# Other rows on the partitions: how the expert weights of a mixture-of-experts layer are laid into SBUF

## The chip, the cores and the metric

The kernel runs on one NeuronCore of one Trainium2 chip. The metric is the time of one execution on the device, in microseconds (us), with all inputs in HBM at the start and all outputs in HBM at the end. Everything is f32.

## The reference, cut to what matters

One layer of a diffusion backbone over 384 tokens of width 1024 (128 context tokens, 256 latent ones). A first half mixes tokens (gated linear attention and differential attention); it is not touched here. The second half is an expert-choice mixture of experts: each of 16 experts takes the 16 context tokens and 32 latent tokens that score highest for it, and runs a SwiGLU of width 2816 on them.

```python
def ec_moe(h, w_router, w_gate, w_up, w_down):
    ...
    aff = jax.nn.softmax((xt @ w_router).astype(jnp.float32), axis=-1)
    cap = CAPACITY_FACTOR * n // N_EXPERTS
    gate, idx = lax.top_k(aff.T, cap)
    xe = jnp.take(xt, idx, axis=0)
    hid = jax.nn.silu(jnp.einsum('ecd,edf->ecf', xe, w_gate)) * jnp.einsum('ecd,edf->ecf', xe, w_up)
    ye = jnp.einsum('ecf,efd->ecd', hid, w_down) * gate[..., None].astype(h.dtype)
    out = jnp.zeros_like(xt).at[idx.reshape(-1)].add(ye.reshape(-1, D))
```

`w_gate` and `w_up` are [16][1024][2816], `w_down` is [16][2816][1024]. Both sums (over d in the first two products, over f in the third) may be taken in any order of their terms, so any row of a weight may lie on any partition, as long as the other operand has the same order.

## The kernel before, in words

The whole layer is one program with hand-written semaphores. Up to about 560 us of the span it does the token mixing, and after it the router. The rest is a loop over the 16 experts; its body is `expert` on PE and on DVE, a loop body on ACT and one on SP, which issues all loads of the weights. The last expert is written out behind the loop on PE and DVE.

**SBUF.** A ring of six quarters, each 2 x 2816 elements on every partition, holds the weights. An expert's gate and up weights are four quarters each, and they take the ring's places 0 to 5 and then 0 and 1 (`(4 * m + q) % 6`). The down weights overwrite places 2 to 5 (from `DOWN0`) once these have been read; they come in four groups (`DOWN_GROUPS`), of 3, 4, 3 and 1 of the 11 pairs of row blocks.

**Loads.** SP (lines 547 to 572) issues the loads in the order in which they are used: gate quarters, up quarters, down groups. Before each it waits until PE has used what lay in its place (`gate_used`, `up_used`, `down_used`). For gate and up (line 536) partition p takes row p * 8 + k of the matrix for k = 0 to 7, quarter q being k = 2q and 2q + 1. For down (line 544) partition p takes row p * 22 + i, for i = 0 to 21. Rows of one partition follow one another in HBM.

**PE for one expert**, `e`:

- L1008: the tokens of the expert are gathered by a product with a 0/1 matrix `sel`. The PE array is used in two halves of 64 columns (`w` = 0, 1); for w = 0 it forms one half of the features of the 48 tokens (64 slots), for w = 1 the other, on the PSUM partitions 64 to 127. Which features are "half w" is said by `h2_half`: those whose index divided by 4 is even or odd. ACT copies the result to `xe`.
- L1013: four transposes turn `xe` (columns `xe_cols[:, i, :]`, every fourth one) to have the features on the partitions. DVE copies the result to `xeT`.
- L1025: gate and up. For each k a stationary operand from `xeT` (128 features x 64 slots) and, for three blocks of columns (4, 4 and 3 times 128, `FCH`) and both halves, a moving operand from the ring. Half w takes the columns with index 2m + w, so the moving operand has a step of two elements. Gate goes to PSUM banks 0 to 2, up to 3 to 5. ACT applies silu to gate (L1297), into `hid`, while up is running; DVE multiplies it by up (L1714), one block after the other, and adds 1 to `hid_done` for each.
- L1033: 11 transposes turn `hid` (columns `hid_cols[:, i, :]`, every eleventh one). PE waits for all three blocks first, since every eleventh column is found in each. ACT copies to `hidT` (L1300).
- L1047: down, 11 x 2 x 2 products over the groups, into banks 6 and 7. DVE scales the result (L1719).
- L1055: the rows go back to their tokens by a product with `selT`; DVE adds them to the sums (L1727), and for the last expert they are added in PSUM, after L999 has brought in the sums so far.

Of the kernel before, what the change touches and what calls it, by code (L numbers as in the profile page):

```python
# [21 lines left out]
P = 128  # L22
D = 1024
KT = D // P
# [3 lines left out]
BANK = 512  # L28
# [164 lines left out]
QUARTER = 2 * FF  # L193
RING = 6 * QUARTER
FT = FF // (2 * P)
# [9 lines left out]
def trunk_layer(nc, x_prompt, x_sample, cache_k, cache_v, st_f, st_b, c, c_ctx, w_mod, b_mod, w_in,  # L205
# [5 lines left out]
    with ExitStack() as ctx:  # L211
# [28 lines left out]
        banks = ctx.enter_context(nc.psum_tensor("banks", [P, 8, BANK], F32))  # L240

        ident = kf[:, 0:P]
# [11 lines left out]
        def reg(a, n):  # L254
            return ring[:, a:a + n]
# [68 lines left out]
        h2 = rows(O4[:])  # L324
# [14 lines left out]
        hid = O2[:, 0:HALF]  # L339
        hidT = O2[:, HALF:2 * HALF].rearrange("p (i n) -> p i n", n=P)  # L340
        sel = O2[:, 2 * HALF:2 * HALF + T * SLOT].rearrange("p (t s) -> p t s", t=T)
        xe = O3[:, 0:BANK]
        xe_cols = xe.rearrange("p (n k) -> p k n", k=4)
        hid_cols = hid.rearrange("p (n i) -> p i n", i=FT)

        def h2_half(t, w):
            return h2[:, t, :].rearrange("p (n w k) -> p w n k", w=2, k=4)[:, w]

        xeT = O3[:, BANK:2 * BANK].rearrange("p (i n) -> p i n", n=P)
        yrow = O3[:, 2 * BANK:4 * BANK]  # L350
        selT = O3[:, 4 * BANK:4 * BANK + NT]
# [102 lines left out]
        hid_done = sem("hidden_ready")  # L454
# [63 lines left out]
        @block.sync  # L518
        def _(sp):
            sp.dma_start(crow[0:8, :], c_ctx.rearrange("(k p) -> k p", p=P)).then_inc(ld_c, 16)  # L520
            sp.dma_start(crow[8:16, :], c.rearrange("b (k p) -> (b k) p", p=P)).then_inc(ld_c, 16)
            sp.dma_start(kf[:], k_f).then_inc(ld_k, 16)
            sp.dma_start(x_r[:, 0, :], x_prompt[0]).then_inc(ld_x[0], 16)
            sp.dma_start(x_r[:, 1:3, :], x_sample[0].rearrange("(t p) d -> p t d", p=P)).then_inc(ld_x[1], 16)
            for n in range(len(WCHUNKS)):
                j = freed_by(SLOT_OF[n], n)
                if j is not None:
                    sp.wait_ge(job_done, j + 1)
                sp.dma_start(w_slot(n), w_chunk(n)).then_inc(wsem[SLOT_OF[n]], 16)

            sp.wait_ge(job_done, J_GB[-1] + 1)
            sp.dma_start(x_r[:, 0, :], x_prompt[0]).then_inc(ld_x2, 16)
            sp.dma_start(x_r[:, 1:3, :], x_sample[0].rearrange("(t p) d -> p t d", p=P)).then_inc(ld_x2, 16)

            def gate_up(w, e, q):
                return gate_v[w][e].rearrange("(p k) f -> p k f", p=P)[:, 2 * q:2 * q + 2, :]

            def quarter(i):
                return reg(i * QUARTER, QUARTER).rearrange("p (k f) -> p k f", k=2)

            def down(e, g):
                a, b = DOWN_GROUPS[g]
                sp.dma_start(reg(DOWN0 + 2 * a * D, 2 * (b - a) * D).rearrange("p (i d) -> p i d", d=D),
                             w_down[0][e].rearrange("(p i) d -> p i d", p=P)[:, 2 * a:2 * b, :]).then_inc(land_d[g], 16)


            wait_family(sp, F_M)
            for q in range(4):
                if q == 3:
                    wait_job_copied(sp, J_WO[-1])  # L550
                sp.dma_start(quarter(q), gate_up(0, 0, q)).then_inc(land_g[q], 16)
            for q in range(4):
                if q >= 2:
                    sp.wait_ge(gate_used, q - 1)
                sp.dma_start(quarter((4 + q) % 6), gate_up(1, 0, q)).then_inc(land_u[q], 16)
            for g in range(4):
                if g == 0:
                    sp.wait_ge(gate_used, 4)
                else:
                    sp.wait_ge(up_used, min(g, 2))  # L560
                down(0, g)
            with sp.Fori(1, NE) as e:

                for q, (used, n) in enumerate(((up_used, 1), (up_used, 0), (down_used, 3), (down_used, 2))):
                    sp.wait_ge(used, e * 4 - n)
                    sp.dma_start(quarter(q), gate_up(0, e, q)).then_inc(land_g[q], 16)
                for q, (used, n) in enumerate(((down_used, -1), (down_used, 0), (gate_used, 1), (gate_used, 2))):
                    sp.wait_ge(used, e * 4 + n)
                    sp.dma_start(quarter((4 + q) % 6), gate_up(1, e, q)).then_inc(land_u[q], 16)
                for g, (used, n) in enumerate(((gate_used, 4), (up_used, 1), (up_used, 2), (up_used, 2))):  # L570
                    sp.wait_ge(used, e * 4 + n)
                    down(e, g)
            for t in range(T):
                sp.wait_ge(f_ready, t + 1)
                dst = y_prompt[0] if t == 0 else y_sample[0, (t - 1) * P:t * P, :]
                sp.dma_start(dst, x_r[:, t, :]).then_inc(stored, 16)
            sp.wait_ge(stored, 16 * T)
            sp.wait_ge(kv_stored, 32)
            sp.wait_ge(gla_st, 16 * 2 * GH)
# [112 lines left out]
        def _(pe):  # L692
# [309 lines left out]
            def expert(e, last=False):  # L1002

                pe.wait_ge(sel_ready, e * T + T)
                pe.wait_ge(acc_done, e * 6 + 6)
                for t in range(T):
                    for w in range(2):
                        x = pe.matmul(banks[64 * w:64 * w + 64, 3, :], sel[:, t, :], h2_half(t, w),  # L1008
                                      start=(t == 0), stop=(t == T - 1))
                x.then_inc(xe_done, 1)  # L1010
                pe.wait_ge(xe_cp, e + 1)
                for i in range(4):
                    x = pe.transpose(banks[:, 4, i * P:(i + 1) * P], xe_cols[:, i, :], ident)  # L1013
                x.then_inc(xet_done, 1)
                pe.wait_ge(xet_cp, e + 1)

                for m, (land, used) in enumerate(((land_g, gate_used), (land_u, up_used))):
                    for q in range(4):
                        pe.wait_ge(land[q], e * 16 + 16)
                        w4 = reg(((4 * m + q) % 6) * QUARTER, QUARTER).rearrange("p (k m w) -> p k w m", k=2, w=2)  # L1020
                        for kk in range(2):
                            k = 2 * q + kk
                            for b, (i0, i1) in enumerate(FCH):
                                for w in range(2):
                                    x = pe.matmul(banks[64 * w:64 * w + 64, 3 * m + b, 0:(i1 - i0) * P],  # L1025
                                                  xeT[:, k % 4, 64 * (k // 4):64 * (k // 4) + 64],
                                                  w4[:, kk, w, i0 * P:i1 * P], start=(k == 0), stop=(k == KT - 1))
                        x.then_inc(used, 1)

                pe.wait_ge(hid_done, e * 3 + 3)  # L1030
                for b, (i0, i1) in enumerate(FCH):
                    for i in range(i0, i1):
                        x = pe.transpose(banks[:, b, (i - i0) * P:(i - i0 + 1) * P], hid_cols[:, i, :], ident)  # L1033
                    x.then_inc(hidt_done, 1)

                if last:
                    rows_so_far(range(3, 6))
                pe.wait_ge(hidt_cp, e * 3 + 3)
                wd = reg(DOWN0, FF // P * D).rearrange("p (i w d) -> p i w d", w=2, d=D)
                for g, (i0, i1) in enumerate(DOWN_GROUPS):  # L1040
                    if last and g == 1:
                        rows_so_far(range(3))
                    pe.wait_ge(land_d[g], e * 16 + 16)
                    for i in range(i0, i1):
                        for dc in range(2):
                            for w in range(2):
                                x = pe.matmul(banks[64 * w:64 * w + 64, 6 + dc, :], hidT[:, i, 64 * w:64 * w + 64],  # L1047
                                              wd[:, i, w, dc * BANK:(dc + 1) * BANK], start=(i == 0), stop=(i == FT - 1))
                    x.then_inc(down_used, 1)

                pe.wait_ge(selT_ready, e + 1)
                pe.wait_ge(y_cp, e * 2 + 2)
                for t in range(T):
                    for dc in range(2):
                        pe.matmul(banks[:, 2 * t + dc, :], selT[:, t * P:(t + 1) * P], yrow[:, dc * BANK:(dc + 1) * BANK],  # L1055
                                  start=not last, stop=True, skip_group_check=last).then_inc(comb_done, 1)
# [715 lines left out]
```

## Time and profile before

| | |
|---|---|
| three runs | 1917.98, 1918.8, 1919.66 us; median 1918.8 |
| the profiled execution | 1917.98 us, span 1916.2 us |
| mean granted clock of TensorE | 0.968 |
| PE busy | 1709.6 us, 89% |
| DMA, all queues | 642.58 MB, mean 335 GB/s over the span |

The span reaches from the first to the last instruction; the time of an execution is 1.8 us longer. In the rows, PE is the matmuls and PEld the loads of their stationary operands, DVE the vector engine, ACT the scalar engine and SPq the queue of SP, which issues the loads. An f32 matmul stands in the trace as two records. "DMA share" is the mean busy share of the core's 16 DMA engines. A packet is one contiguous run that one of them moves; each DMA ends with 16 small ones that write its semaphore, which the view counts under 512 B.

### The profile page before, as it was taken

To read this page: it belongs to the slowest core of one execution; us is meant where nothing else is said; L and a number is where in the kernel's file an instruction comes from. 1 tells how busy PE (TensorE), PEld (TensorE's weight loads), DVE (VectorE), ACT (ScalarE), POOL (GpSimd) and SP (SyncE) were. 2 spreads that over 40 slices of the span, in tenths; PEclk is the share of its full clock that TensorE was granted. 3 is DMA by queue.
4 is the path that set the end of the run, shared out by engine and by line. 5 is a ranking of instruction groups with operands and counts; after the bars stand their busy time and mean duration, and the time that the engine had idled before them with its cause. 6 is when DMAs were issued, how large, how long until landed. Compare 5 with 4: busy or idle time off the path is not lost.

```text
span 1916.2 us, 18332 instructions
## 1 busy us (share of the span) xinstructions
PE 1709.6 (89%) x7569; PEld 797.6 (42%) x7569; DVE 502.9 (26%) x934; ACT 282.7 (15%) x557; POOL 85.6 (4%) x136
## 2 busy tenths in 40 slices
PE   4899997999996989989999888998889989889996
PEld 1446776777764333333333233332333333333332
DVE  2166566776447010110101101011010110101103
ACT  1221132445213010001000000000000000000000
POOL 3001031112001000000000000000000000000000
PEclk9999998999998999999999999999999999999999
DMA  8683243314466799999999999999999999999995
GB/s 280 251 292 89 71 127 99 88 45 136 144 246 257 319 429 431 431 431 433 426 431 431 431 430 429 430 432 431 431 428 428 432 432 432 428 430 430 431 428 213
DMA packets 59479, 642.58 MB, mean 335 GB/s; under 512 B 4929, under 2 KB 5073, under 8 KB 31793
## 3 DMA queue, kind: packets, MB, share of 16 engines
q1 hardware_dynamic: 55232, 629.83, 79.4%
q0 software_dynamic: 4208, 12.24, 2.0%
q8 instruction: 25, 0.41, 0.1%
q14 instruction: 14, 0.11, 0.0%
HBM read 638.34 MB, written 3.71 MB: 335 GB/s over the span
## 4 chain that ended last, share of the span: by engine, by line
PE 66%; DMA 22%; DVE 8%; issue 2%; ACT 1%; SPq 0%; POOL 0%; DVEq 0%; ACTq 0%
PE banks L1025 24%; DMA ring<-in_w_exp_down 15%; PE banks L754 13%; PE banks L1047 11%; PE banks L1055 4%; DMA ring<-in_w_exp_up 4%; PE banks L760 3%; PE banks L1008 2%; PE banks L728 2%; DMA ring<-in_w_mod 2%; PE banks L882 1%; DVE slot_parts L1471 1%; PE banks L811 1%; DMA ring<-in_w_in 1%; DVE O L1719 1%
## 5 line engine op out<-in xcount | busy, mean ns | idle before, releaser
L1025 PE MATMUL banks<-ring,O 128*64 128x512 f32 (+1 forms) x3072 | 640.2, 575 | 28.2 <-DMA ring<-in_w_exp_up 14.5
L1025 PEld LDWEIGHTS banks<-ring,O 128*64 128x64 f32 x3072 | 229.1, 134 | 431.1 <-issue 403.0
L1047 PE MATMUL banks<-ring,O 128*64 128x512 f32 x1408 | 328.1, 623 | 24.3 <-DMA ring<-in_w_exp_down 14.4
L1047 PEld LDWEIGHTS banks<-ring,O 128*64 128x64 f32 x1408 | 101.8, 144 | 241.0 <-issue 194.9
L1714 DVE TENSOR_TENSOR O<-O,banks 128x512 f32<-128x512 f32 (+1 forms) x48 | 28.0, 639 | 651.6 <-PE banks L1025 651.6
L754 PE MATMUL banks<-slot_parts,X_parts 128*128 128x512 f32 x576 | 161.3, 421 | 9.6 <-issue 9.6
L1719 DVE TENSOR_TENSOR O<-banks,O 128x512 f32<-128x512 f32 x32 | 20.6, 686 | 388.6 <-PE banks L1047 388.6
L754 PEld LDWEIGHTS banks<-slot_parts,X_parts 128*128 128x128 f32 x576 | 107.4, 194 | 35.6 <-issue 10.4
L1055 PE MATMUL banks<-O 128*128 128x512 f32 x192 | 86.6, 601 | 22.4 <-DVE O L1719 22.4
L760 PE MATMUL banks<-ring,H 128*128 128x512 f32 x192 | 84.5, 595 | 0.0
L1471 DVE TENSOR_TENSOR slot_parts<-ring,slot_parts 128x512 fp32r<-128x512 f32 x128 | 81.0, 689 | 4.0 <-ACT slot_parts L1094 2.8
L1294 ACT ACTIVATE O<-banks 128x512 f32<-128x512 f32 x16 | 9.6, 597 | 470.1 <-PE banks L1008 470.1
L754 PE MATMUL banks<-slot_parts,H_parts 128*128 128x512 f32 x288 | 78.7, 390 | 0.0
L1300 ACT ACTIVATE O<-banks 128x512 f32<-128x512 f32 (+1 forms) x48 | 24.4, 560 | 355.7 <-PE banks L1033 355.5
L1297 ACT ACTIVATE O<-banks 128x512 f32<-128x512 f32 (+1 forms) x48 | 23.5, 563 | 327.0 <-PE banks L1025 327.0
L1727 DVE TENSOR_TENSOR X<-X,banks 128x512 f32<-128x512 f32 x90 | 61.8, 687 | 31.2 <-PE banks L1055 31.2
L1055 PEld LDWEIGHTS banks<-O 128*128 128x128 f32 x192 | 35.2, 190 | 74.7 <-issue 40.6
L754 PEld LDWEIGHTS banks<-slot_parts,H_parts 128*128 128x128 f32 x288 | 54.1, 188 | 11.7
L1008 PE MATMUL banks<-O 128*64 128x512 f32 x192 | 47.3, 629 | 12.4 <-DVE X L1727 11.8
L1033 PE MATMUL banks<-kf,O 128*128 128x128 f32 x176 | 29.4, 324 | 31.1 <-DVE O L1714 31.1
L760 PEld LDWEIGHTS banks<-ring,H 128*128 128x128 f32 x192 | 35.8, 190 | 45.8 <-issue 45.8
L728 PE MATMUL banks<-H,ring 128*128 128x384 f32 x128 | 45.1, 510 | 6.0 <-DMA ring<-in_w_in 5.9
(256 smaller groups left out, 1169.2 us busy)
## 6 DMA issues: line engine op xcount, KB each, us to landing
ring<-in_w_exp_gate SPq DMA_DIRECT2D x64, 2816.0 KB, 30.3
ring<-in_w_exp_up SPq DMA_DIRECT2D x64, 2816.0 KB, 26.1
ring<-in_w_exp_down SPq DMA_DIRECT2D x32, 3072.0 KB, 23.5
ring<-in_w_exp_down SPq DMA_DIRECT2D x16, 4096.0 KB, 28.1
ring<-in_w_in SPq DMA_DIRECT2D x16, 2048.0 KB, 9.8
ring<-in_w_mod SPq DMA_DIRECT2D x12, 2048.0 KB, 15.4
ring<-in_w_exp_down SPq DMA_DIRECT2D x16, 1024.0 KB, 32.4
ring<-in_w_proj_a SPq DMA_DIRECT2D x2, 2048.0 KB, 7.8
```

Source lines behind the costliest of these rows:

```text
L728: x = pe.matmul(out[:, 0:NT], w[:, k, i * P:(i + 1) * P], hT[:, k, :], start=(k == 0), stop=(k == KT - 1))
L754: x = pe.matmul(out, a[:, k, i * P:(i + 1) * P], w[:, k, :], start=(n == 0 and k == 0), stop=(n == 2 and k == KT - 1))
L760: x = pe.matmul(out, src[:, k, i * P:(i + 1) * P], w[:, k, :], start=(k == 0), stop=(k == KT - 1))
L1008: x = pe.matmul(banks[64 * w:64 * w + 64, 3, :], sel[:, t, :], h2_half(t, w), start=(t == 0), stop=(t == T - 1))
L1025: x = pe.matmul(banks[64 * w:64 * w + 64, 3 * m + b, 0:(i1 - i0) * P], xeT[:, k % 4, 64 * (k // 4):64 * (k // 4) + 64], w4[:, kk, w, i0 * ...
L1033: x = pe.transpose(banks[:, b, (i - i0) * P:(i - i0 + 1) * P], hid_cols[:, i, :], ident)
L1047: x = pe.matmul(banks[64 * w:64 * w + 64, 6 + dc, :], hidT[:, i, 64 * w:64 * w + 64], wd[:, i, w, dc * BANK:(dc + 1) * BANK], start=(i == ...
L1055: pe.matmul(banks[:, 2 * t + dc, :], selT[:, t * P:(t + 1) * P], yrow[:, dc * BANK:(dc + 1) * BANK], start=not last, stop=True, skip_group ...
L1471: dve.tensor_tensor(low[:, k, :], w[:, k, :], high[:, k, :].bitcast(F32), ALU.subtract).then_inc(w_split, 1)
L1714: dve.tensor_tensor(hid[:, i0 * P:i1 * P], hid[:, i0 * P:i1 * P], banks[:, 3 + b, 0:(i1 - i0) * P], ALU.mult).then_inc(hid_done, 1)
L1719: dve.tensor_tensor(yrow[:, cs], banks[:, 6 + dc, :], g2s[:, cs], ALU.mult).then_inc(y_cp, 1)
L1727: dve.tensor_tensor(dst, dst, banks[:, n, :], ALU.add).then_inc(acc_done, 1)
```

## The change

The rows of the expert weights are laid on the partitions the other way round: row k * 128 + p of gate and up on partition p, and row i * 128 + p of down. With it every operand that has to follow that order changes: half w of the features is w * 512 to w * 512 + 511; `xe` and `hid` are transposed in blocks of 128 contiguous columns; of gate and up's columns half w takes the blocks of 128 with an even or odd number. As a block of `hid` columns is complete now when its own product is done, PE waits for the three products one by one, each just ahead of the transposes that need it.

```diff
-        xe_cols = xe.rearrange("p (n k) -> p k n", k=4)
-        hid_cols = hid.rearrange("p (n i) -> p i n", i=FT)
-
-        def h2_half(t, w):
-            return h2[:, t, :].rearrange("p (n w k) -> p w n k", w=2, k=4)[:, w]
...
             def gate_up(w, e, q):
-                return gate_v[w][e].rearrange("(p k) f -> p k f", p=P)[:, 2 * q:2 * q + 2, :]
+                return gate_v[w][e].rearrange("(k p) f -> p k f", p=P)[:, 2 * q:2 * q + 2, :]
...
-                             w_down[0][e].rearrange("(p i) d -> p i d", p=P)[:, 2 * a:2 * b, :]).then_inc(land_d[g], 16)
+                             w_down[0][e].rearrange("(i p) d -> p i d", p=P)[:, 2 * a:2 * b, :]).then_inc(land_d[g], 16)
...
-                        x = pe.matmul(banks[64 * w:64 * w + 64, 3, :], sel[:, t, :], h2_half(t, w),
+                        x = pe.matmul(banks[64 * w:64 * w + 64, 3, :], sel[:, t, :], h2[:, t, w * BANK:(w + 1) * BANK],
                                       start=(t == 0), stop=(t == T - 1))
...
-                    x = pe.transpose(banks[:, 4, i * P:(i + 1) * P], xe_cols[:, i, :], ident)
+                    x = pe.transpose(banks[:, 4, i * P:(i + 1) * P], xe[:, i * P:(i + 1) * P], ident)
...
-                        w4 = reg(((4 * m + q) % 6) * QUARTER, QUARTER).rearrange("p (k m w) -> p k w m", k=2, w=2)
+                        w4 = reg(((4 * m + q) % 6) * QUARTER, QUARTER).rearrange("p (k i w n) -> p k i w n", k=2, w=2, n=P)
...
-                                                  w4[:, kk, w, i0 * P:i1 * P], start=(k == 0), stop=(k == KT - 1))
+                                                  w4[:, kk, i0:i1, w, :], start=(k == 0), stop=(k == KT - 1))
...
-                pe.wait_ge(hid_done, e * 3 + 3)
                 for b, (i0, i1) in enumerate(FCH):
+                    pe.wait_ge(hid_done, e * 3 + b + 1)
                     for i in range(i0, i1):
-                        x = pe.transpose(banks[:, b, (i - i0) * P:(i - i0 + 1) * P], hid_cols[:, i, :], ident)
+                        x = pe.transpose(banks[:, b, (i - i0) * P:(i - i0 + 1) * P], hid[:, i * P:(i + 1) * P], ident)
```

## Rows read from the trace of the kernel before

**Rows 1.** The page: DMA share and rate in 40 slices, packets, chain by engine.

```profile
DMA  8683243314466799999999999999999999999995
GB/s 280 251 292 89 71 127 99 88 45 136 144 246 257 319 429 431 431 431 433 426 431 431 431 430 429 430 432 431 431 428 428 432 432 432 428 430 430 431 428 213
DMA packets 59479, 642.58 MB, mean 335 GB/s; under 512 B 4929, under 2 KB 5073, under 8 KB 31793
...
PE 66%; DMA 22%; DVE 8%; issue 2%; ACT 1%; SPq 0%; POOL 0%; DVEq 0%; ACTq 0%
```

**Rows 2.** Windows: stretch, length, busy of PE, PEld, DVE, ACT, POOL; clock, DMA share, GB/s.

```profile
214.50:221.50 7.00, 7.00 (x38) 5.37 (x38) 0.97 (x4) 2.10 (x7) 0.00 (x0) 1.00 0.97 282
499.30:504.30 5.00, 4.80 (x19) 3.51 (x20) 1.11 (x2) 0.00 (x0) 0.00 (x0) 1.00 1.01 385
...
700.00:1870.00 1170.00, 1047.71 (x4686) 378.24 (x4686) 129.56 (x237) 89.48 (x131) 0.00 (x0) 0.98 1.00 430
...
1880.00:1890.00 10.00, 10.00 (x40) 3.45 (x42) 0.00 (x0) 0.00 (x0) 0.00 (x0) 1.00 0.83 352
```

**Rows 3.** Timeline of ACT, the copy of `xe` in four experts: start, duration, idle before.

```profile
785.74 0.60 ACT L1294 ACTIVATE O<-banks 128x512 f32<-128x512 f32 x1 [28.29 <-PE banks L1008]
861.62 0.60 ACT L1294 ACTIVATE O<-banks 128x512 f32<-128x512 f32 x1 [28.29 <-PE banks L1008]
...
1342.32 0.60 ACT L1294 ACTIVATE O<-banks 128x512 f32<-128x512 f32 x1 [31.16 <-PE banks L1008]
1422.73 0.60 ACT L1294 ACTIVATE O<-banks 128x512 f32<-128x512 f32 x1 [30.72 <-PE banks L1008]
```

**Rows 4.** Waits over 700 to 1850 us: in total, times, longest.

```profile
PEld banks L1047 <- DMA ring<-in_w_exp_down: 32.2, 22, 3.1
...
PEld banks L1025 <- DMA ring<-in_w_exp_up: 24.4, 21, 2.2
```

**Rows 5.** DMA view of 501 to 504, 547.8 to 549.8 and 1100 to 1180 us.

```profile
DMA packets 587, 1.20 MB, mean 401 GB/s; under 512 B 0, under 2 KB 0, under 8 KB 587
...
DMA packets 202, 0.82 MB, mean 408 GB/s; under 512 B 3, under 2 KB 3, under 8 KB 202
...
DMA packets 1719, 34.40 MB, mean 430 GB/s; under 512 B 192, under 2 KB 192, under 8 KB 192
```

**Rows 6.** Timeline of PE: the first gate matmuls, and the last expert's end.

```profile
633.54 39.83 PE L1025 MATMUL banks<-ring,O 128*64 128x512 f32 x192 [0.86 <-DVE O L1705]
...
1863.45 5.18 PE L1025 MATMUL banks<-ring,O 128*64 128x512 f32 x24 [1.38 <-DMA ring<-in_w_exp_up]
...
1882.67 13.95 PE L1047 MATMUL banks<-ring,O 128*64 128x512 f32 x64
```

**Rows 7.** Timeline of all engines, 1141 to 1180 us, one expert from up to the next.

```profile
1141.50 0.14 PEld L1025 LDWEIGHTS banks<-ring,O 128*64 128x64 f32 x2 [0.31 <-issue]
1141.84 0.14 PEld L1025 LDWEIGHTS banks<-ring,O 128*64 128x64 f32 x2 [0.20 <-issue]
...
1144.97 1.75 DVE L1714 TENSOR_TENSOR O<-O,banks 128x512 f32<-128x512 f32 x3 [41.28 <-PE banks L1025]
...
1146.78 1.61 PE L1033 MATMUL banks<-kf,O 128*128 128x128 f32 x11 [1.95 <-DVE O L1714]
1147.57 1.47 ACT L1300 ACTIVATE O<-banks 128x512 f32<-128x512 f32 x3 [22.60 <-PE banks L1033]
...
1149.09 5.37 PE L1047 MATMUL banks<-ring,O 128*64 128x512 f32 x24 [0.70 <-ACT O L1300]
...
1150.43 0.14 PEld L1047 LDWEIGHTS banks<-ring,O 128*64 128x64 f32 x2 [0.29 <-issue]
...
1179.90 2.79 PE L1008 MATMUL banks<-O 128*64 128x512 f32 x12 [0.78 <-DVE X L1727]
```

**Rows 8.** Lines by form, 700 to 1850 us: busy and mean ns of a weight load.

```profile
L1055 PEld LDWEIGHTS banks<-O 128*128 128x128 f32 x180 | 33.0, 190 | 70.0 <-issue 35.9 <-DVE O L1719 34.1
...
L1033 PEld LDWEIGHTS banks<-kf,O 128*128 128x128 f32 x154 | 21.6, 215 | 37.1 <-DVE O L1714 37.1
```

## The prediction, made before the changed kernel was run

> **What bounds the kernel now.** I read the page first, for where the time goes. Expert loads fill the last two thirds of the span: the DMA digits stand at 9 from slice 17 on and the rate stays at 426 to 433 GB/s. But the page's chain gives PE 66% of the span and DMA 22% [rows 1], so the page alone can't say which of the two sets the pace. The windows answer it: over 700 to 1870 us the 16 DMA engines are busy for a share of 1.00 at 430 GB/s, and PE for 1047.71 of 1170 us, 90% [rows 2]. A queue that is never empty is a bound; an engine that rests for a tenth isn't.
>
> The starts of the ACT copy of `xe`, one for each expert, check it [rows 3]. From 785.74 to 861.62 an expert takes 75.88 us: the loads are still ahead from the start and PE sets the pace. From 1342.32 to 1422.73 it takes 80.41 us. An expert's weights are 3 x 1024 x 2816 x 4 bytes = 34.60 MB, and 34.60 MB at 430 GB/s is 80.5 us. So after the first few experts the loads set the period, and PE, which needs 75.9, waits 4.5 us for them in each. The waits name them: `in_w_exp_down` and `in_w_exp_up` before L1047 and L1025, 32.2 and 24.4 us on the weight loads [rows 4]. What shortens PE's work inside an expert is worth nothing there; what lengthens a load is paid in full.
>
> **The packets.** The number of bytes and of DMA issues does not change. What changes is the length of a contiguous run in HBM, and so the number of packets. Before, partition p reads rows p*8+2q and p*8+2q+1 of gate or up, which lie one behind the other: one packet of 22.5 KB. Afterwards it reads row k*128+p for two k: two packets of 11 KB. For down, partition p reads 6, 8, 6 or 2 rows in one piece now (24, 32, 24, 8 KB, by `DOWN_GROUPS`) and afterwards that many pieces of 4 KB. An engine serves 8 partitions, so per expert: gate and up go from 64 to 128 packets per engine, down from 32 to 176. That is 208 more, 64 and 144.
>
> The trace of before shows what a packet costs beyond its bytes. Dense stretches [rows 5]: in 1100:1180 there are 1719 packets less 192 completion writes, so 1527 of 22.5 KB on average; 16 engines x 80 us / 1527 = 838 ns each. In 501:504 587 packets of 2 KB, so 81.8 ns each, 401 GB/s. In 547.8:549.8 199 of 4 KB, so 160.8 ns each, 408 GB/s. A line through the 2 KB and the 22.5 KB point has 36.9 ns per KB of 1000 bytes and leaves 6.2 ns per packet; one through the 4 KB and the 22.5 KB point leaves 10.3 ns. These are my bounds for one more packet in a full queue. I take 7 ns, near the 2 KB row, which rests on three times as many packets. An expert then takes 208 x 7 ns = 1.5 us longer (1.3 to 2.1).
>
> The Trainium skill gives a smaller price (DMA: Bandwidth & Descriptors, section Why small descriptors are slow): about 3 cycles per packet beside one cycle for each 32 bytes. By that an 11 KB packet loses 0.4% more than a 22.5 KB one and a 4 KB packet 2% more than a long one, 0.8 us per expert, and the end would come near 1928 us. The rows at 2 and 4 KB ask for more than that, and I go by them.
>
> **Where the extra time counts.** The stream runs without a gap from the release of the first gate quarter of expert 0 at about 638 us (PE starts on it at 633.54 [rows 6], and a quarter of gate or up takes it 5 us). The six quarters loaded before that were waiting in any case. Up to the last up quarter of expert 15, which PE waits for at 1863.45 [rows 6], it holds 122 quarters and 15 downs: 122 x 8 + 15 x 144 = 3136 more packets on each engine. 3136 x 7 ns = 22.0 us (19.4 to 32.3).
>
> **What PE gains.** Four edits, all for PE.
> - L1025's moving operand has a step of two elements now; afterwards it is four runs of 128. The trace has two records for each f32 matmul, and their weight loads come in pairs. Two pairs stand 0.14 + 0.31 = 0.45 us apart for 512 columns and 0.14 + 0.20 = 0.34 for 384, against 0.14 + 0.29 = 0.43 for 512 at L1047, whose operand is contiguous [rows 7]; 384 would be 0.32 at that pace. Per k there are four such steps of 512 and two of 384: 6 x 0.02 = 0.12, x 16 (8 k, gate and up) = 1.9 us per expert. The last up quarter holds two of the 16 k: 0.25 us.
> - `hid_done` is waited for block by block. Now PE stands still while DVE multiplies three blocks: DVE starts at 1144.97, the transposes at 1146.78, ACT's first copy at 1147.57, the down matmuls at 1149.09 [rows 7]. With the first block turned at once, the transposes start after one product of 0.69 us, about 1145.7; they run behind DVE and ACT's copies (1.47 us together) behind them, the last block is ready at 1146.72, turned by 1147.4 and copied by 1148.1. That is 0.95 us earlier.
> - `hid_cols` (step 11) and `xe_cols` (step 4) become contiguous. Loads for the transposes take 215 ns against 190 for the 128-column loads of L1055 [rows 8], so 15 x 0.025 = 0.4 us at most; 0.2 of it behind the last up load, nothing below.
> - `h2_half` reads groups of four now and halves afterwards. Its 12 records take 2.79 us as they are [rows 7], the pace of a contiguous operand; nothing.
> Sum 3.1 to 3.3 us: PE would need 72.8 in place of 75.9 per expert. In the period this is hidden by the loads; PE only waits longer, 9 us instead of 4.5. It shows twice. At the start, the first quarter is released 0.25 us sooner. At the end, the chain from the last up quarter to the last down matmul is PE work alone, 1863.45 to 1882.67 + 13.95 = 1896.6 [rows 6], with no wait for down: 0.25 + 0.95 + 0.2 = 1.4 us shorter. Down has to be there in time: the stream ends near 1888 (352 GB/s in 1880:1890 is 3.5 MB, then empty [rows 2]). Afterwards it ends at 1888.2 + 22.0 + 1.0 - 0.25 = 1911, while PE wants the last group 1.8 us before 1917, at 1915. It is still hidden, with 4 us to spare; at 10 ns per packet too.
>
> **Sum.** 22.0 - 0.25 - 1.4 = +20.3 us. The profiled execution took 1917.98 us for a span of 1916.2, so 1938.3; the median of the runs is 0.8 above that execution. I say 1938.5 us, 1.0% slower.
>
> **Rivals.**
> A. Packets cost nothing in a full queue: the reads of the next packet start while the last is written, and only bytes count. For it: the DMA share is a little over 1 in dense stretches, 1.01 at 2 KB [rows 2], so packets do overlap. Against: the spacing worked out above has that overlap in it already, and it is still 5 to 7% wide of the long packets' rate. It would give -1.7 us, 1917. By the rule of the Trainium skill that 512 bytes are enough for line rate (DMA: Bandwidth & Descriptors, Specifications) this is what should come; the rows at 2 KB and 4 KB disagree.
> B. PE is the bound, as its 66% of the chain suggests, and its 3.1 us per expert come off: 15 x 3.1 = 47 us, 1871. It decides only where the loads of an expert take less than PE's 75.9 us; at 80.4 that is far. The first five experts, where PE did set the pace, only hand their time back to the wait for the loads.
> C. HBM reads adjacent rows faster, since a whole DMA is one stretch of 1.4 or 0.5 to 1 MB afterwards. It would have to bring 430 GB/s to over 437 before the packets' price is taken off to turn the sign (20.3 of some 1250 us are 1.6%); at 440 it ends near 1910. Against it: `in_w_proj_a` has neighbouring partitions 4 KB apart, and such loads reach 385 to 401 GB/s [rows 2, 5].
> D. The new order of rows collides in HBM. `in_w_in` runs at 282 GB/s over 7 us where loads of the same size from `in_w_proj_b` and `in_w_out` make 385 [rows 2], so the layout in HBM can cost. If only down fell to 385 GB/s, 11.5 MB would take 30.0 in place of 26.8 us: 3.2 per expert in place of my 1.0, 1971 in all; at 282 GB/s 2135. Against it: down's pitch afterwards is that of `in_w_proj_a` and the loads of x, which ran dense at 401 and 408.
> PE's clock is a smaller matter: its granted mean is 0.98 [rows 2], more waiting may halve it more often, and there are 9 us of room in each period. In the last 33 us one stretch of a few us at half speed costs 2 to 3.
>
> **How the numbers follow.** The forecast with its bounds: from half the lower price (3 ns, should the 2 KB stretch hold gaps of its own) to the upper one and 3 us for the clock, so 9.4 - 1.7 to 32.3 - 1.7 + 3 on 1918: 1926 to 1951, chance 0.74. A 0.10 (1914 to 1922), B 0.02, C 0.05, D and anything else above 1951 0.09. A measurement of this kernel tells 0.2%, 3.8 us, from no change. Slower is all of the forecast and D; A is mostly within 0.2%; B and C are faster: 0.84, 0.09, 0.07. The range 1924 to 1951 leaves out A, B, C and D: at most 2 in 10, the forecast's own edge of 2 us with them.
>
> **What would show it.** DMA packets about 112,700 in place of 59,479 [rows 1] (3328 more on each of 16 engines); the share still 1.00 from 700 us on, with 420 to 425 GB/s in place of 430; 81.9 us between `xe` copies in the middle; L1025's loads 0.43 apart; PE's waits for `in_w_exp_down` and `in_w_exp_up` doubled; the wait before L1033 down from 1.95 to under 1 us. I am wrong if the rate stays at 430 (A), passes 437 (C), or falls under 415 (D), or if PE still takes 75.9 us where it isn't waiting for a load.

## The result, and the profile after

The changed kernel takes 1948.4 us (median of 4 runs, 1946.3 to 1949.2), the kernel before in the same job 1918.5. The ratio is 1.0152, 95% interval 1.0138 to 1.0167: 29.9 us slower, where 20 were forecast.

The page of the changed kernel, the lines that answer to [rows 1]:

```profile
span 1946.4 us, 18362 instructions
...
DMA  8673242224285899999999999999999999999995
GB/s 275 252 292 94 61 135 82 87 56 159 105 313 221 350 426 416 423 420 417 425 416 424 418 419 423 417 426 416 420 422 417 425 416 421 420 417 426 416 422 220
DMA packets 112726, 642.58 MB, mean 330 GB/s; under 512 B 4928, under 2 KB 5072, under 8 KB 76848
...
PE 66%; DMA 25%; DVE 6%; issue 2%; ACT 1%; SPq 0%; DVEq 0%; ACTq 0%
```

DMA stands at 9 from slice 17 on as before, and the rate under them is 416 to 426 GB/s instead of 426 to 433. The bytes are the same to the last digit, the packets are nearly twice as many. The chain still gives PE 66%; it was no sign of the bound before and is none now.

Windows of the changed kernel, columns as in [rows 2]:

```profile
700.00:1870.00 1170.00, 1002.65 (x4548) 357.00 (x4548) 125.10 (x229) 88.76 (x128) 0.00 (x0) 0.97 1.01 420
...
1910.00:1920.00 10.00, 9.43 (x39) 2.98 (x39) 0.00 (x0) 0.00 (x0) 0.00 (x0) 1.00 0.99 394
1920.00:1930.00 10.00, 8.52 (x36) 2.88 (x33) 1.29 (x2) 0.00 (x0) 0.00 (x0) 1.00 0.03 14
```

PE is busy for 45 us less in the same 1170 us [rows 2], and the end comes later all the same. About half of the 45 is work that now lies outside the window, as each expert takes 2.4% longer (25 of 1047.71 us); the rest is what the edits saved. The stream of loads ends at about 1919.4 (394 GB/s over the last full window, at 420 while it ran), where it ended near 1888 before.

Timeline of ACT in the changed kernel, the copy of `xe` in experts 0, 1, 2 and 15 (as [rows 3]):

```profile
632.17 0.60 ACT L1288 ACTIVATE O<-banks 128x512 f32<-128x512 f32 x1 [9.12 <-PE banks L1002]
705.09 0.60 ACT L1288 ACTIVATE O<-banks 128x512 f32<-128x512 f32 x1 [28.29 <-PE banks L1002]
784.65 0.60 ACT L1288 ACTIVATE O<-banks 128x512 f32<-128x512 f32 x1 [34.35 <-PE banks L1002]
...
1855.83 0.60 ACT L1288 ACTIVATE O<-banks 128x512 f32<-128x512 f32 x1 [34.69 <-PE banks L1002]
```

From expert 2 on the loads set the period: (1855.83 - 784.65) / 13 = 82.40 us against 80.41 [rows 3]. The 208 further packets of an engine cost 1.99 us, 9.6 ns each. The 80.41 is one period; ten of them in the kernel before give (1825.00 - 1020.65) / 10 = 80.44, and with that it is 9.4 ns:

```profile
1020.65 0.60 ACT L1294 ACTIVATE O<-banks 128x512 f32<-128x512 f32 x1 [30.24 <-PE banks L1008]
...
1825.00 0.60 ACT L1294 ACTIVATE O<-banks 128x512 f32<-128x512 f32 x1 [31.34 <-PE banks L1008]
```

Expert 0 took 72.92 us, the 72.8 that PE was expected to need; the lead of the loads, which lasted four experts before, is gone within expert 1.

DMA view of the changed kernel over 1303 to 1313 us (gate or up, 11 KB) and 1321 to 1331 us (down, 4 KB):

```profile
DMA packets 396, 4.27 MB, mean 427 GB/s; under 512 B 17, under 2 KB 17, under 8 KB 17
...
DMA packets 1016, 4.10 MB, mean 410 GB/s; under 512 B 16, under 2 KB 16, under 8 KB 1016
```

Less the completion writes that is 16 x 10 us / 379 = 422 ns for 11 KB and 16 x 10 / 1000 = 160.0 ns for 4 KB. The 4 KB row of [rows 5] had said 160.8. One packet more or less in so short a window moves these spacings by 1.1 and 0.2 ns, so the price of a packet is better read from the periods.

Waits of the changed kernel over 700 to 1850 us (as [rows 4], and the wait ahead of the transposes, 37.1 us in [rows 8]):

```profile
PEld banks L1041 <- DMA ring<-in_w_exp_down: 72.8, 16, 5.3
...
PEld banks L1019 <- DMA ring<-in_w_exp_up: 47.6, 27, 2.5
...
PEld banks L1027 <- DVE O L1708: 24.3, 28, 1.6
```

Both waits for weights have doubled: PE's saved time is in them. Timeline of the changed kernel at the hand-over from up to down, and at the end:

```profile
1305.76 0.15 PEld L1019 LDWEIGHTS banks<-ring,O 128*64 128x64 f32 x2 [0.28 <-issue]
...
1306.94 0.15 PEld L1019 LDWEIGHTS banks<-ring,O 128*64 128x64 f32 x2 [0.17 <-issue]
...
1322.55 1.75 DVE L1708 TENSOR_TENSOR O<-O,banks 128x512 f32<-128x512 f32 x3 [40.96 <-PE banks L1019]
1323.29 0.42 PEld L1027 LDWEIGHTS banks<-kf,O 128*128 128x128 f32 x4 [1.56 <-DVE O L1708]
1323.30 1.61 PE L1027 MATMUL banks<-kf,O 128*128 128x128 f32 x11 [0.89 <-DVE O L1708]
...
1325.62 5.37 PE L1041 MATMUL banks<-ring,O 128*64 128x512 f32 x24 [0.71 <-ACT O L1294]
...
1335.38 15.54 PE L1041 MATMUL banks<-ring,O 128*64 128x512 f32 x64 [4.40 <-DMA ring<-in_w_exp_down]
...
1894.11 4.94 PE L1019 MATMUL banks<-ring,O 128*64 128x512 f32 x24 [1.84 <-DMA ring<-in_w_exp_up]
...
1903.96 5.37 PE L1041 MATMUL banks<-ring,O 128*64 128x512 f32 x24
...
1919.69 7.09 PE L1041 MATMUL banks<-ring,O 128*64 128x512 f32 x32 [0.57 <-DMA ring<-in_w_exp_down]
```

Pairs of weight loads stand 0.15 + 0.28 = 0.43 and 0.15 + 0.17 = 0.32 us apart; from DVE's start to the first down matmul it is 3.07 us, 4.12 in [rows 7]. PE won in the loop what it was to win, and stood still for 4.40 us a little later.

### The profile page after: what moved, and what is told of

The parts are those of the page before. It is cut to its first block, busy times and chain, and to the rows that moved or that the text cites. A ratio compares the mean times of both kernels' runs of the same rounds, so it can differ in the third digit from the quotient of the medians.

```text
span 1946.4 us, 18362 instructions
## 1 busy us (share of the span) xinstructions
PE 1689.8 (87%) x7569; PEld 784.7 (40%) x7569; DVE 502.7 (26%) x934; ACT 283.5 (15%) x557; POOL 85.6 (4%) x136
## 2 busy tenths in 40 slices
DMA packets 112726, 642.58 MB, mean 330 GB/s; under 512 B 4928, under 2 KB 5072, under 8 KB 76848
## 3 DMA queue, kind: packets, MB, share of 16 engines
q1 hardware_dynamic: 108480, 629.83, 80.4%
## 4 chain that ended last, share of the span: by engine, by line
PE 66%; DMA 25%; DVE 6%; issue 2%; ACT 1%; SPq 0%; DVEq 0%; ACTq 0%
DMA ring<-in_w_exp_down 23%; PE banks L1019 21%; PE banks L1041 13%; PE banks L748 13%; PE banks L754 4%; PE banks L1049 4%; PE banks L1002 2%; PE banks L722 2%; DMA ring<-in_w_mod 2%; PE banks L876 1%; PE banks L716 1%; DVE slot_parts L1465 1%; PE banks L805 1%; DMA ring<-in_w_in 1%; DVE O L1713 1%
## 5 line engine op out<-in xcount | busy, mean ns | idle before, releaser
L1019 PE MATMUL banks<-ring,O 128*64 128x512 f32 (+1 forms) x3072 | 613.8, 558 | 46.8 <-DMA ring<-in_w_exp_up 33.1
L1041 PE MATMUL banks<-ring,O 128*64 128x512 f32 x1408 | 340.2, 643 | 71.2 <-DMA ring<-in_w_exp_down 60.5
L748 PEld LDWEIGHTS banks<-slot_parts,X_parts 128*128 128x128 f32 x576 | 107.6, 194 | 35.6 <-issue 10.3
L695 PE MATMUL banks<-kf,O 128*128 128x128 f32 x144 | 25.5, 303 | 21.3 <-DVE O L1388 12.6
```

The lines of the kernel that those rows point to most:

```text
L695: x = pe.transpose(banks[:, 2 + b % 2, i * P:(i + 1) * P], src, ident)
L748: x = pe.matmul(out, a[:, k, i * P:(i + 1) * P], w[:, k, :], start=(n == 0 and k == 0), stop=(n == 2 and k == KT - 1))
```

## Experiments

Three theories for the 30 us. One: each packet has a fixed price in a queue that is never empty. Two: HBM gives adjacent rows more slowly, and the cost goes with the bytes so read. Three: SP's queue is blocked. The last came from the trace. The issues of down by their line, first in the kernel before (a timeline row, and the durations in ns, least, median and most), then in the changed one:

```profile
1364.62 10.89 SPq L543 DMA_DIRECT2D ring<-in_w_exp_down  x4
...
L543 SPq DMA_DIRECT2D ring<-in_w_exp_down x64: 327/333/432, 653.6 to 1857.8; - x64
```

```profile
1300.39 28.34 SPq L537 DMA_DIRECT2D ring<-in_w_exp_down  x4
...
L537 SPq DMA_DIRECT2D ring<-in_w_exp_down x64: 368/1654/11936, 653.5 to 1898.7; - x64
```

From the first to the end of the last, the four issues of an expert take 28 us instead of 11 (most of the 11 is waiting between them), and a single one lasts up to 11.9 us where 0.43 was the most.

The differences below are the stated ratio applied to some 1920 us. The kernel before moved by one or two us from job to job (medians 1918.5 to 1920.3), and among the profiled executions the first copy of `xe` starts anywhere between 630.1 and 634.4 us, before any of the edits can act; a difference of 1 or 2 us in one profile is within that. The period between copies of `xe` does not depend on where the experts begin.

### The rows of gate and up alone

```diff
-                return gate_v[w][e].rearrange("(p k) f -> p k f", p=P)[:, 2 * q:2 * q + 2, :]
+                return gate_v[w][e].rearrange("(k p) f -> p k f", p=P)[:, 2 * q:2 * q + 2, :]
```
with `h2[:, t, w * BANK:(w + 1) * BANK]` and `xe[:, i * P:(i + 1) * P]` as the operands that follow from it.

> The new row order for gate and up alone (with the operands h2 and xe that must follow it); down as before. Theory 1, a fixed price per packet in a queue that is never empty: the two profiles give (82.38 - 80.41) us / 208 packets = 9.5 ns. Here 64 more packets per engine and expert: period 81.0 us, 976 packets x 9.5 ns = 9.3 us in all, 1928 us. Theory 2, the order of rows in HBM costs by the byte: gate and up are two thirds of the bytes and take two thirds of the 30 us, 1938 us. Theory 3, the descriptors of down that block SP's queue (issues of up to 11.9 us) are the cause: nothing here, 1918 us.

1929.5 us, ratio 1.0044 (1.0027 to 1.0061), 8.4 us (9.2 by the medians). Timeline of ACT (copies of `xe` seven experts apart) and of SP:

```profile
1188.24 0.60 ACT L1294 ACTIVATE O<-banks 128x512 f32<-128x512 f32 x1 [31.16 <-PE banks L1008]
...
1755.39 0.60 ACT L1294 ACTIVATE O<-banks 128x512 f32<-128x512 f32 x1 [31.16 <-PE banks L1008]
...
1292.74 10.89 SPq L543 DMA_DIRECT2D ring<-in_w_exp_down  x4
```

The period is 81.02 us, 0.61 for 64 packets: 9.5 ns (0.58 and 9.1 ns from 80.44). Two thirds of the bytes in the new order made less than a third of the loss, so theory two falls by its size. SP's issues of down take 10.89 us as before (and none of gate and up lasts over 0.40), and the loss is there, so theory three explains no part of this.

### The down side alone

Everything else of the change: `(i p) d` for down, the column blocks, the contiguous transposes and the waits for `hid_done` block by block.

> The rest of the change alone: down in 4 KB rows, the new column blocks, contiguous transposes, the wait for hid block by block; gate and up rows as before. Theory 1 (price per packet, 9.5 ns): 144 more per engine and expert, period 81.8 us, 15 x 144 x 9.5 ns = 20.5 us, less 1.7 for PE at start and end, plus 0.6 for the last down group: 1938 us. Theory 2 (bytes in the new order): one third of 30 us, 1928 us. Theory 3 (SP blocked by down's descriptors): the whole 30 us, 1948 us.

1939.3 us, ratio 1.0097 (1.0081 to 1.0114), 18.6 us. Timeline of ACT, seven experts apart:

```profile
1112.37 0.60 ACT L1294 ACTIVATE O<-banks 128x512 f32<-128x512 f32 x1 [34.52 <-PE banks L1008]
...
1684.86 0.60 ACT L1294 ACTIVATE O<-banks 128x512 f32<-128x512 f32 x1 [34.60 <-PE banks L1008]
```

The period is 81.78 us, 1.37 for 144 packets: 9.5 ns (9.3 from 80.44). The two halves of the change give 8.4 + 18.6 = 27.0 us; the whole gave 29.9, within the three intervals.

### PE's edits with the old loads

All edits of the change except the two load patterns. The products are of rows that don't belong together; their number and size are those of the kernel.

> All of PE's edits with the loads of the kernel before, so the operands don't belong to one another and the products are of other rows; the work is the same in size. Theory 1: the loads keep their 80.4 us per expert, PE needs 3 us less and waits 3 us more in each; only the start (0.25) and the end (1.4) show, 1916.8 us. Rival: PE sets the pace after all, 15 x 3 us less, 1873 us. Rival of the other sign: longer waits halve PE's clock more often, or the faster releases order the loads worse: above 1920 us.

1917.1 us, ratio 0.9981 (0.9972 to 0.9991): 3.6 us less, with 1.7 to 5.4 in the interval, where 1.6 was expected. Timeline of PE at its end, and of ACT eight experts apart:

```profile
1866.79 4.95 PE L1025 MATMUL banks<-ring,O 128*64 128x512 f32 x24 [0.92 <-DMA ring<-in_w_exp_up]
...
1884.72 13.95 PE L1047 MATMUL banks<-ring,O 128*64 128x512 f32 x64
...
1106.63 0.60 ACT L1294 ACTIVATE O<-banks 128x512 f32<-128x512 f32 x1 [34.80 <-PE banks L1008]
...
1749.03 0.60 ACT L1294 ACTIVATE O<-banks 128x512 f32<-128x512 f32 x1 [33.69 <-PE banks L1008]
```

The last stretch, 1866.79 to 1898.67, is 31.9 us against 33.2 [rows 6]: 1.3 of the 3.6. The period is 80.30, the loads' own. PE is busy for 1022 of the 1170 us from 700 on, 25 less than before [rows 2]. So 3 us of PE's work per expert are worth next to nothing while the loads fill the queue, and PE is not the bound. Where the other 2 us are is open; they are the size of the spread between executions, and the profiled one, at 1920.1 us, is among the slower.

### Short packets in the old order

```diff
-                sp.dma_start(reg(DOWN0 + 2 * a * D, 2 * (b - a) * D).rearrange("p (i d) -> p i d", d=D),
-                             w_down[0][e].rearrange("(p i) d -> p i d", p=P)[:, 2 * a:2 * b, :]).then_inc(land_d[g], 16)
+                for i in range(2 * a, 2 * b):
+                    sp.dma_start(reg(DOWN0 + i * D, D),
+                                 w_down[0][e].rearrange("(p i) d -> p i d", p=P)[:, i, :]).then_inc(land_d[g], 16)
```

> The kernel before with its own row order, down issued as 22 DMAs of one row per partition: 4 KB packets whose neighbours on the next partition lie 88 KB away, and 22 completion writes per engine in place of 4. Theory 1 (price per packet): 15 x 144 x 9.5 ns = 20.5 us and 15 x 18 writes x 9 ns = 2.4 us, 1941 us, period 81.9 us. Theory 2 (the new order of rows costs, not the packets): 1918 to 1921 us. Theory 3: SP's queue blocks by descriptors, so it blocks here as well; not told apart from theory 1.

1939.6 us, ratio 1.0100 (1.0083 to 1.0117), 19.2 us. Timeline of ACT five experts apart, and the window of 1100 to 1260 us:

```profile
1355.40 0.60 ACT L1296 ACTIVATE O<-banks 128x512 f32<-128x512 f32 x1 [32.00 <-PE banks L1009]
...
1764.31 0.60 ACT L1296 ACTIVATE O<-banks 128x512 f32<-128x512 f32 x1 [32.43 <-PE banks L1009]
...
1100.00:1260.00 160.00, 142.93 (x624) 51.68 (x626) 17.16 (x32) 12.64 (x18) 0.00 (x0) 0.96 1.01 423
```

This is the run that decides. Nothing of the order of rows or of PE's operands is changed; the runs are cut to 4 KB, with neighbours 88 KB apart. It takes 22 DMAs where down had 4, and PE waits for all of a group's. The period is 81.78 us and the rate 423 GB/s, as with the down side in the new order. As the down side alone had this period with 4 DMAs, the number of DMAs and the 18 further completion writes of an engine don't show beside that.

### The same rows, cut once more

The changed kernel with each down group in two DMAs of 512 columns each, 2 KB packets.

> The changed kernel with each down group issued as two DMAs, one for each half of the columns: 2 KB packets in place of 4 KB, the same rows on the same partitions. Theory 1 (9.5 ns for each further packet of an engine, whatever its length): 176 more per engine and expert, period 84.0 us, 16 x 176 x 9.5 ns = 27 us on the changed kernel's 1948.4: 1975 us. Rival: the cost is not in the number but in where runs begin in HBM or how long they are (the step from 24 KB to 4 KB has paid it): 1948 us, or far more than 1990 us if packets of 2 KB run as slowly as those of w_in did at 282 GB/s.

1974.1 us, 25.7 above the changed kernel's 1948.4, which is from another job (ratio to the kernel before 1.0286, 1.0270 to 1.0302). Timeline of ACT eight experts apart, and the DMA view over 1163 to 1173 us, while down runs:

```profile
1124.12 0.60 ACT L1290 ACTIVATE O<-banks 128x512 f32<-128x512 f32 x1 [36.91 <-PE banks L1004]
...
1796.46 0.60 ACT L1290 ACTIVATE O<-banks 128x512 f32<-128x512 f32 x1 [36.99 <-PE banks L1004]
...
DMA packets 1927, 3.87 MB, mean 387 GB/s; under 512 B 38, under 2 KB 38, under 8 KB 1927
```

Period 84.04 us, 1.64 more for 176 packets: 9.3 ns. The price is the same, within 0.3 ns, from 4 to 2 KB as from 24 to 4. It is a price of the packet and not of its length.

### Fewer packets than before

The kernel before with gate and up in halves for the experts in the middle (`[:, 4 * h:4 * h + 4, :]`, four rows of a partition, 45 KB in one run); SP waits for both places of a half.

> The kernel before with gate and up loaded in halves (four rows of a partition, 45 KB in one run) for experts 1 to 14 and for gate of expert 15; up of expert 15 and all of expert 0 stay in quarters. If a packet can be that long, 32 packets less per engine and expert, 472 in all; by theory 1 at 9.5 ns period 80.1 us and 4.5 us less than before. If the hardware cuts the run at some length (the longest packet seen is 32 KB), no change in the count or 0 gain. Rival: a coarser ring leaves DMA without work or PE waiting for a half at the end: slower than before by 5 us or more.

1917.5 us, ratio 0.9991 (0.9982 to 1.0000). 2 us less instead of 4.5, and with an interval that touches one it is unclear on its own. The packets by the page, two windows of this run, and PE in expert 14:

```profile
DMA packets 51127, 642.57 MB, mean 336 GB/s; under 512 B 4001, under 2 KB 4145, under 8 KB 30865
...
1100.00:1260.00 160.00, 140.62 (x638) 50.35 (x636) 17.20 (x32) 12.20 (x18) 0.00 (x0) 0.99 1.00 432
...
1880.00:1890.00 10.00, 10.00 (x50) 3.41 (x48) 0.00 (x0) 0.00 (x0) 0.00 (x0) 1.00 0.32 134
...
1778.16 10.14 PE L1043 MATMUL banks<-ring,O 128*64 128x512 f32 x48 [1.30 <-DMA ring<-in_w_exp_up]
```

A run of 45 KB goes as one packet: 58 DMAs of 128 runs in place of twice as many are 7424 packets less, with 58 x 16 completion writes 8352, which is 59,479 - 51,127. Per engine that is 464 packets; the expectation had counted 472. The rate has risen to 432 GB/s and the stream ends near 1883 instead of 1888 (134 GB/s over 10 us are 3.1 us at 430). In this execution the experts had begun 1.1 us earlier than in the one of before (the first copy of `xe` at 630.14 us, not 631.28), so some 4 of the 5 us are the loads', about what 464 packets should save. PE didn't take all of them: it waited 1.30 us for a whole half in expert 14, and in expert 15 it no longer waited for the last up quarter, so that the loads were ahead of it at the end.

### Halves, and the changed down side for the last expert

As the last run, and for expert 15 alone down in 4 KB rows with the column blocks and the waits block by block, where PE's stretch after the last up quarter is on the path.

> The run before this one, and for expert 15 alone the changed order of the down side (down in 4 KB rows, column blocks, the waits for hid block by block). Theory 1: the packets of the last down lie behind PE's own work and cost at most 0.3 us, PE's last stretch is 1.3 us shorter: 1.0 to 1.3 us below the run before this one. Rival: the last down lands late, as in the changed kernel (0.57 us of wait), and eats the gain.

1916.7 us, ratio 0.9983 (0.9974 to 0.9992): 3.3 us less than the kernel before, and the interval leaves out one. It is a gain of under 0.2%. Against the run with halves it is 0.9 us, close to the 1.0 to 1.3 expected, but the two intervals overlap. Timeline of PE at its end:

```profile
1861.55 4.95 PE L1044 MATMUL banks<-ring,O 128*64 128x512 f32 x24 [0.18 <-DMA ring<-in_w_exp_up]
...
1887.11 7.09 PE L1070 MATMUL banks<-ring,O 128*64 128x512 f32 x32 [0.55 <-DMA ring<-in_w_exp_down]
```

The rival named there is real too: PE waits 0.55 us for the last down groups, which takes back part of the 1.3.

### Up of expert 14 in quarters as well

> As the run with halves and the changed end, but up of expert 14 comes in quarters too. In the runs with halves the stream of loads ended 5 us sooner (about 1883 in place of 1888) and the time fell by 2 to 3 only, because PE, which had waited for a whole half in expert 14, was behind and no longer waited for the last up quarter or only for 0.18 us. Theory 1 with that reading: PE is through expert 14 earlier, the wait before the last up quarter comes back (0.5 us or more), the time falls by up to 2.5 us more, to about 0.3% below the kernel before. Rival: the loss of 2 us lay elsewhere (the coarser releases): no further gain, 0.15%.

1916.1 us, ratio 0.9981 (0.9972 to 0.9991), no different from the last run. The profiled execution, at 1920.4 us well above the median of its own runs, has the wait back. Timeline of PE:

```profile
1864.75 6.64 PE L1045 MATMUL banks<-ring,O 128*64 128x512 f32 x24 [2.13 <-DMA ring<-in_w_exp_up]
```

The wait that the reading asked for came, the time it promised didn't, and the wait is weak support. In this execution the experts began 3.8 us later than in the one with halves (first copy of `xe` at 633.94 us, not 630.14), and the stream of loads ran on to about 1891 us (406 GB/s over 1880 to 1890, 30 over the ten after), so the last up quarter came late in any case. Nor did the stream end near 1883 in both runs with halves, as the expectation has it: in the second it ended near 1888 (320 GB/s over 1880 to 1890). Whether PE's lateness was what ate the 2 us of the run with halves stays open.

## Why the prediction was right

**The bound.** Right. Share 1.00 before and 1.01 after, periods of 80.4 and 82.4 us that are the bytes over the rate, and PE's edits alone moving the period by 0.1 us.

**The packets.** Their number was right: 3328 more on each of 16 engines are 53,248, and the page counts 112,726 - 59,479 = 53,247. The price was the term that was mis-sized: 7 ns where the periods give 9.4 to 9.6, 9.5 below. Both bounds, 6.2 and 10.3, held it. The choice between them was wrong. I took the 2 KB row because it rests on more packets; the 4 KB row was of the kind of packet that down was to get, and said 160.8 ns where the changed kernel has 160.0. The 2 KB row was not only short: packets of 2 KB with the same layout in HBM stand 16 x 10 us / 1889 = 84.7 ns apart in the expert loop of the run with 2 KB packets, and 81.8 in [rows 5]. Why the loads of the projection matrices run 3 ns closer is open; that window holds only 37 packets of each engine, and one more or less on every engine would be 2.2 ns. With 9.5 ns the sum is 3136 x 9.5 = 29.8, less 1.65: +28.1, against 29.9 measured. The end, below, gave 0.5 where 1.4 was counted, which makes it 29.0, and in the profiled execution the experts began 0.9 us later than before (632.17 after 631.28), within the scatter. So the mechanism held and the range held the time, but by its upper bound: the sum of 20.3 was a third short, and a price of 10.3 ns would have been as defensible from [rows 5].

The Trainium skill's three cycles beside a cycle per 32 bytes (DMA: Bandwidth & Descriptors, Why small descriptors are slow) would be, as an estimate from that page, 3 of 131 parts of a 4 KB packet, 3.7 ns. The 32 bytes of descriptor that the section adds make it 4 of 132, 4.8 ns. The runs show about twice that, and the measurement decides.

**What PE gains.** Right in its sum, 72.92 us for expert 0 where 72.8 was said. (Expert 0 of the kernel before took 78.61, not 75.9: over 673 to 711 us its granted clock was 0.91, and the 11 transposes there lasted 2.62 us in place of 1.61. The changed kernel has 1.00 over 673 to 706. Loads that set the period later on take up such a difference.) Its parts: matmul steps of 0.43 and 0.32 as expected; from DVE's product to down 1.05 us less where I had 0.95 and 0.2 apart; the transposes' loads take 140 ns now, not the 190 of other 128-column loads, but 11 transposes still take 1.61 us [rows 7], so the loads were not what held them.

**The end.** From the last up quarter to the first down matmul of expert 15 it is 9.85 us where it was 11.15. But I had the last down hidden with 4 us to spare, and PE waits 0.57 us for it at 1919.69. With that wait the whole stretch, 1894.11 to 1919.69 + 7.09, is 32.67 us against 33.17 [rows 6]: 0.5 gained, not 1.4. The wait comes with the group before the last, 7 us before PE is through, and I had asked only for the last one, 1.8 us before. And I let data count as landed when the stream ends. By the rate the stream ended at about 1919.4, but the group before the last landed at 1919.7 with 1 MB still behind it, and the last one at 1922.1 (issued at 1886.7 and 1898.7, landing 33.0 and 23.4 us later), 2.7 us after that end. The dearer packets add only 144 x 2.5 ns = 0.4 us to this.

**The rivals.** A, no price for packets, falls: a period of 81.02 us for gate and up alone and of 81.78 for down by row, where only the runs are shorter. B falls with PE's edits alone. C and D, the order of rows in HBM for better or worse, fall together: the period is 81.78 us, and the mean rate over whole experts 423 GB/s, with down in 4 KB packets whether neighbours are 4 or 88 KB apart. For gate and up no run parts the order from the packets, but their price comes out the same, 9.1 to 9.5 ns, with nothing left for the order that these runs could tell. (The 2 KB row of [rows 5] is of `in_w_proj_b`, which SP issued at 497.31 us, not of `in_w_proj_a`; both are laid out alike.) The clock of PE, 0.97 over 700 to 1870 us after 0.98, had room and cost nothing that can be told.

## What to carry to other kernels

Where the queue of loads is never empty, count packets, not only bytes: with each partition's rows in one piece the same 34.6 MB took 80.4 us, in pieces of 4 and 11 KB 82.4. An edit that makes an operand contiguous on the compute side is paid for by the loads if it breaks up their runs, and is worth nothing to an engine that then waits for them. To price what the trace doesn't show yet, take the row most like it in kind, not the one with the most samples.

## What the runs showed of the hardware

Spacing of packets on one engine in full queues: 2 KB 84.7 ns, 4 KB 160.0, 11 KB 422, 22.5 KB 838. All lie within 2.5 ns of 9 ns + 36.9 ns per 1000 bytes, and 16 engines at 36.9 ns are 434 GB/s, which agrees with the ceiling of 435 in the Trainium skill (DMA: Bandwidth & Descriptors, Where 436 GB/s comes from). The same section has loads from HBM bound at some 358 instead; the 430 measured here are well above that, and the measurement decides. The price of a packet is thus some 9 ns at any length between 2 and 22 KB, and 5.6% of a 4 KB one. What an engine does in these 9 ns no run shows. The runs of 45 KB fit it as well: 2046 packets of 33.8 KB on average in 1100 to 1260 us of the run with halves are 1251 ns each, where the line has 1256.

An issue on SP of a DMA with many short runs lasts up to 11.9 us while the queue is full (the changed kernel; 0.43 at most before), and holds back what is issued behind it. It cost nothing that shows here: the price per packet is 9.1 to 9.5 ns where SP wasn't held up (gate and up alone) and 9.3 to 9.5 where it was (down by row, issues of up to 6.1 us).

A moving f32 operand with a step of two elements costs 5% of a matmul's pace (0.45 against 0.43 us between pairs of records of 512 columns; 24 records of the last up quarter take 5.18 us with it and 4.95 without). By the Trainium skill (SBUF — State Buffer, Door 1: The DMA port swizzle) two accesses in a line of 16 bytes should be at full speed; here they are nearly so.
